# VectorE instead of GpSimd for the low parts of weight units in the dilated attention

## The chip, the cores and the metric

The kernel runs on one core of a Trainium2 chip. The metric is the time of one execution on the device, in microseconds (us). The kernel before took 3922.28 us, the median of three runs (3920.53 to 3923.07).

## The reference, cut to what matters

The program is two transformer blocks one after the other. The change lies in the second layer of the first block, the dilated mixture attention: for 512 tokens, 16 heads of width 64 and three dilations (1, 4, 16) it computes

```python
qkv = (h @ w_qkv).reshape(b, s, N_GROUPS_B, 3, H_B, HEAD_DIM)
# per dilation group: softmax attention in a band, with a distance bias per head
o, lse = banded_attention(q, k, v, slopes, dil, win // (2 * dil), BLOCK_B)
# mixture of the three groups by the softmax of their log denominators
wts = jax.nn.softmax(jnp.stack(lses), axis=0)
o = jnp.einsum('gbsh,gbshd->bshd', wts, jnp.stack(outs).astype(jnp.float32))
return o.astype(h.dtype).reshape(b, s, H_B * HEAD_DIM) @ w_out
```

The kernel takes the three groups together in one softmax over 768 keys: 512 of the first group, 128 each of the other two. All products with weights are of float32 quality: each operand is split in a high part (rounded to the type fp32r) and a low part (the rest), and a product is three matmuls, high by high, low by high and high by low.

## The kernel before, in words

Weights come from HBM in units of 128 x 2048 numbers (1 MB). `Weights.feed` on the SyncE queue loads them into a ring of four buffers; a buffer is loaded again when the unit in it is used up (`used`). Of each unit ScalarE writes the high part to one of two buffers (`write_hi`, L71), and GpSimd writes the low part, ring minus high part, in place over the ring buffer (`write_lo`, L76). TensorE waits for the low part (`parts`), which implies the high part.

The stage "att_b" (`attention_stage` with a `project`) does two things at once. It projects queries and keys for 8 pairs of heads: 6 chunks a pair, a chunk being 24 matmuls of 512 columns (8 blocks, three products each, L122 to L124) into PSUM bank 7. A unit holds 2 chunks, so a pair takes 3 units and the stage 24. VectorE copies each chunk out of bank 7 with scaling (`ProjectB.copy`, L828 for even chunks, L830 for odd ones), and TensorE may not begin the next chunk before that copy (`pair_chunk_copied`), since there is one bank. And it does the softmax attention of 32 items, 4 to a pair (a pair of heads and one residue tile of 128 queries).

The chunks of pair 0 stand ahead of the items (the prologue). While the 4 items of pair p run, the 6 chunks of pair p+1 are laid between them: 0 and 1 in item 0 of the pair, 2 in item 1, 3 and 4 in item 2, 5 in item 3 (`chunks_after`). The items of the last pair have no chunks beside them.

The order on each engine is fixed by the program. In step i:

- TensorE: scores of item i (L674), values of item i-3 (L656), a chunk, transposes of half 0 of item i-2 (L644), the second chunk if there is one, transposes of half 1.
- VectorE: bias and maximum of both halves of item i (L718), the negated maximum (L721), reciprocal and scaling of item i-1 (L697, L701), copy of the output of item i-3 (L706), then the copies of the chunks.
- ScalarE: the exponentials of item i (L744), the high part of the unit after the one that an even chunk uses (`unit_of`), the copies of the transposed probabilities of item i-2 (L759).
- GpSimd: nothing but the 24 low parts, in a loop of its own: each waits only for its high part.

Of the kernel before, what the change touches and what calls it, by code (L numbers as in the profile page):

```python
# [559 lines left out]
def attention_stage(nc, c, w, items, name, sink, project=None):  # L560
# [13 lines left out]
    with ExitStack() as ctx:  # L574
# [15 lines left out]
        def S(i, half):  # L590
            return c.bank[2 * half + i % 2] if DEEP == 2 else c.wide[half]
# [4 lines left out]
        def chunks_after(i):  # L596

            if not project or i >= N:
                return []
            pair, j = i // in_pair + 1, i % in_pair  # L600
            at = [n for n in range(per) if n * in_pair // per == j]
            return [(pair, n) for n in at] if pair < pairs else []

        def unit_of(pair, j):

            n = (pair * per + j) // 2 + 1
            return n if j % 2 == 0 and n < project.units else None

        with nc.Block() as block:
            if project:  # L610
                @block.sync
                def _(sp):
                    w.feed(sp, project.units)

            if project:
                @block.gpsimd
                def _(pool):
                    for n in range(project.units):
                        w.write_lo(pool, hi_ready, lo_ready, 0, n)

            @block.tensor
            def _(pe):
                def pair_chunk(pair, j):
# [63 lines left out]
            @block.vector  # L687
            def _(dve):
                def scale_of(i):

                    dve.wait_ge(prob_ready, 2 * i + 2)
                    if sink is not None:
                        dve.wait_ge(sunk_ready, i + 1)
                        dve.tensor_tensor(total[:, i, :], den[:, i, :], sunk[:, i, :], ALU.add).then_inc(total_ready, 1)
                        dve.wait_ge(total_ready, i + 1)
                    src = den if sink is None else total
                    dve.reciprocal(rden[:, i, :], src[:, i, :]).then_inc(rden_ready, 1)  # L697
                    dve.wait_ge(rden_ready, i + 1)
                    keys = items[i].keys
                    for half in HALVES:  # L700
                        dve.tensor_scalar(prob[:, i % SB, half, 0:keys], prob[:, i % SB, half, 0:keys], rden[:, i, half:half + 1], None,  # L701
                                          ALU.mult).then_inc(prob_scaled, 1)

                def copy_out(i):
                    dve.wait_ge(out_done, i + 1)
                    dve.tensor_copy(items[i].out, O[:, 0:P]).then_inc(out_copied, 1)  # L706

                for j in range(per):
                    project.copy(dve, w, 0, j, pair_chunk_done, pair_chunk_copied)
                for i in range(N + LAG + 1):  # L710
                    if i < N:
                        it = items[i]
                        dve.wait_ge(scores_done, i + 1)
                        if i >= SB:

                            dve.wait_ge(turned, 2 * (i - SB) + 2)
                        for half in HALVES:
                            dve.tensor_tensor_reduce(prob[:, i % SB, half, 0:it.keys], S(i, half)[:, 0:it.keys], it.dist, -it.slopes[half],  # L718
                                                     -3e38, ALU.add, ALU.max, top[:, i, half:half + 1]).then_inc(biased, 1)
                        dve.wait_ge(biased, 2 * i + 2)  # L720
                        dve.tensor_scalar(negtop[:, i, :], top[:, i, :], -1.0, None, ALU.mult).then_inc(negtop_ready, 1)  # L721
                        if sink is not None:
                            at = it.heads[0]
                            dve.tensor_tensor(sunk[:, i, :], sink[:, at:it.heads[1] + 1:it.heads[1] - at], top[:, i, :],
                                              ALU.subtract).then_inc(sink_shifted, 1)
                    if 0 <= i - LAG + 1 < N:
                        scale_of(i - LAG + 1)
                    if i >= LAG + 1:
                        copy_out(i - LAG - 1)
                    for chunk in chunks_after(i):  # L730
                        project.copy(dve, w, *chunk, pair_chunk_done, pair_chunk_copied)

            @block.scalar
# [2188 lines left out]
def first_block(nc, c, w, a, x, upto, dump):  # L2922
    with ExitStack() as first:
# [4 lines left out]
        with ExitStack() as layer:  # L2928
            def sl(n, shape):
                return layer.enter_context(nc.sbuf_tensor(n, shape, F32))  # L2930
            q, k_, v, o = sl("q_a", [P, DC, T]), sl("k_a", [P, 2, T]), sl("v_a", [P, TT, 2 * P]), sl("o_a", [P, DC, T])
            dist, sink, scale = sl("dist_a", [P, 3 * P]), sl("sink", [P, HEADS]), sl("q_scale_a", [P, DC])
            project_a_stage(nc, c, w, h, x, COLS["norm_mix0"], q, k_, v, (scale[:, :], a["q_scale_a"]),
                            [(dist[:, :], a["dist_a"]), (sink[:, :], a["sink"].partition_broadcast(P))])
            attention_stage(nc, c, w, attention_a_items(q, k_, v, dist, o), "att_a", sink)
            out_stage(nc, c, w, o, h, x, "out_a")
# [5 lines left out]
        with ExitStack() as layer:  # L2942
            def sl(n, shape, dt=F32):
                return layer.enter_context(nc.sbuf_tensor(n, shape, dt))
            v = sl("v_b", [P, 3, TT, D])

            kept, o = nc.dram_tensor("x_kept", [P, DC, T], F32, kind="Internal").ap(), x
            qk = [sl(f"qk{i}", [P, 6, T]) for i in range(2)]
            dist, scale = sl("dist_b", [P, TT, T + 2 * P], mybir.dt.bfloat16), sl("q_scale_b", [P, DC])
            values_b_stage(nc, c, w, h, x, COLS["norm_mix1"], v,  # L2950
                           (dist[:, :, :], a["dist_b"]), [(scale[:, :], a["q_scale_b"]), (kept, x[:, :, :])])
            attention_stage(nc, c, w, attention_b_items(qk, v, dist, o), "att_b", None, ProjectB(c, h, qk, scale))
            out_stage(nc, c, w, o, h, x, "out_b", kept)
# [231 lines left out]
```

## Time and profile before

| | |
|---|---|
| median of three runs | 3922.28 us |
| the profiled execution's own time | 3915.05 us |
| its span, first to last instruction | 3913.0 us |
| TensorE busy | 3301.5 us, 84% |
| VectorE busy | 1998.2 us, 51% |
| ScalarE busy | 1310.5 us, 33% |
| GpSimd busy | 927.4 us, 24% |
| mean granted TensorE clock | 0.898 of full |
| the stage att_b | from about 793.6 to 1272 us of the span |

The shares are averages over many stages with different limits. Matmuls are pipelined: a row shows about 0.40 us for one of 512 columns, while in a stream at full clock one starts every 0.23 us. In a timeline row the figures are start, duration, engine, line and operation; in brackets stands the idle time of the engine just before it and who ended it.

### The profile page before, as it was taken

Reading aid. Unit: us, or ns where it says so; the run is one execution under the profiler, and the core shown is the slowest. Engines: PE = TensorE matmul, PEld = TensorE weight load, DVE = VectorE, ACT = ScalarE, POOL = GpSimd, SP = SyncE. Lnnn points to the kernel's source line nnn. Section 1 sums busy time; section 2 is a strip of 40 time slices with the busy share of each in tenths; the row PEclk is TensorE's granted clock in tenths of the full one; section 3 lists DMA queues with packets and bytes.
Section 4 is the critical chain, followed back from the end, with each engine's and each line's share of the span. In section 5 each row is a group of like instructions: output and inputs, shape, how many; then the busy total and the mean of one; then the engine's idle time right before and its main releaser. Section 6 shows DMA issues by size and latency. Waiting matters only on the chain. (4 is left out here: it accounts for less than half of the span.)

```text
span 3913.0 us, 53828 instructions
## 1 busy us (share of the span) xinstructions
PE 3301.5 (84%) x21896; PEld 2576.2 (66%) x21896; DVE 1998.2 (51%) x2721; ACT 1310.5 (33%) x1631; POOL 927.4 (24%) x485
## 2 busy tenths in 40 slices
PE   7789999989998799988599688439998747999994
PEld 5468877967776588753387576228887336888882
DVE  3755523023333565220498244656554327999994
ACT  2633222223333333210322101422212116777772
POOL 2034433332220344310122100000100003435540
PEclk9989999999999899998799755559999868999996
DMA  3012223221110222227011000130011117999993
GB/s 123 12 64 89 95 86 124 86 75 56 55 65 33 76 97 96 86 99 264 25 65 54 4 1 8 43 136 24 24 46 66 43 47 267 357 370 372 370 363 122
DMA packets 75667, 439.22 MB, mean 112 GB/s; under 512 B 15148, under 2 KB 16300, under 8 KB 26708
## 3 DMA queue, kind: packets, MB, share of 16 engines
q1 hardware_dynamic: 65716, 426.97, 29.6%
q0 software_dynamic: 9760, 9.47, 0.7%
q8 instruction: 148, 2.42, 0.3%
q14 instruction: 43, 0.35, 0.0%
HBM read 419.47 MB, written 37.89 MB: 117 GB/s over the span
## 5 line engine op out<-in xcount | busy, mean ns | idle before, releaser
L76 POOL TENSOR_TENSOR ring_lo<-ring,unit_hi 128x2048 fp32r<-128x2048 f32 x116 | 537.0, 4631 | 1170.9 <-ACT unit_hi L71 1170.9
L122 PE MATMUL wide<-h_hi,unit_hi 128*128 128x512 f32 x1296 | 521.3, 402 | 89.6 <-DVE h_lo L182 44.0
L124 PE MATMUL wide<-h_hi,ring_lo 128*128 128x512 f32 x1296 | 520.0, 401 | 0.0
L123 PE MATMUL wide<-h_lo,unit_hi 128*128 128x512 f32 x1296 | 519.3, 401 | 0.0
L2642 DVE TENSOR_TENSOR ex_w_lo<-ring,ex_w_hi 128x2048 fp32r<-128x2048 f32 x192 | 437.4, 2288 | 45.2 <-ACT ex_w_hi L2597 43.8
L2597 ACT CAST ex_w_hi<-ring 128x2048 fp32r<-128x2048 f32 x192 | 365.9, 1911 | 110.8 <-DMA ring<-in_weights 102.3
L71 ACT CAST unit_hi<-ring 128x2048 fp32r<-128x2048 f32 x116 | 220.4, 1900 | 462.1 <-PE wide L124 453.7
L122 PEld LDWEIGHTS wide<-h_hi,unit_hi 128*128 128x128 f32 x1296 | 251.4, 194 | 168.5 <-POOL ring_lo L76 60.1
L123 PEld LDWEIGHTS wide<-h_lo,unit_hi 128*128 128x128 f32 x1296 | 247.6, 191 | 53.4 <-issue 0.2
L124 PEld LDWEIGHTS wide<-h_hi,ring_lo 128*128 128x128 f32 x1296 | 247.3, 191 | 53.4
L383 DVE TENSOR_TENSOR ffn_hidden_lo<-ffn_whole,ffn_hidden_hi 128x512 f32 (+1 forms) x44 | 201.5, 4581 | 50.5 <-ACT ffn_hidden_hi L358 50.5
L2541 PE MATMUL wide<-ex_w_hi,ex_x_hi 128*128 128x512 f32 x512 | 204.6, 400 | 10.4 <-DVE ex_x_lo L2647 10.0
L2543 PE MATMUL wide<-ex_w_hi,ex_x_lo 128*128 128x512 f32 x512 | 201.1, 393 | 0.0
L2542 PE MATMUL wide<-ex_w_lo,ex_x_hi 128*128 128x512 f32 x512 | 200.6, 392 | 0.0
L122 PE MATMUL wide<-in_hi,in_unit_hi 128*128 128x512 f32 (+3 forms) x424 | 147.6, 348 | 34.5 <-POOL ring_lo L76 34.5
L2500 POOL TENSOR_TENSOR ex_held<-ex_blank 128x1 f32<-128x1 f32 x64 | 89.8, 1403 | 320.0 <-DVE ex_results L2668 317.5
L1204 DVE SCALAR_TENSOR_TENSOR conv<-grid,cols,conv 128x512 f32<-128x512 f32 x160 | 158.2, 989 | 3.5
L122 PE MATMUL wide<-ffn_hidden_hi,unit_hi 128*128 128x512 f32 x352 | 141.0, 400 | 14.4 <-issue 14.4
L124 PE MATMUL wide<-in_hi,ring_lo 128*128 128x512 f32 (+3 forms) x424 | 146.4, 345 | 0.0
L124 PE MATMUL wide<-ffn_hidden_hi,ring_lo 128*128 128x512 f32 x352 | 141.0, 401 | 0.0
L123 PE MATMUL wide<-ffn_hidden_lo,unit_hi 128*128 128x512 f32 x352 | 140.4, 399 | 0.0
L2001 DVE COPY_PREDICATED rw_X<-level_mask,wide 128x256 f32<-128x256 uint32 x120 | 53.2, 443 | 148.2 <-PE wide L1857 147.7
(492 smaller groups left out, 6528.7 us busy)
## 6 DMA issues: line engine op xcount, KB each, us to landing
ring<-in_weights SPq DMA_DIRECT2D x356, 1024.0 KB, 5.6
factors<-rf_out SPq DMA_DIRECT2D x8, 1536.0 KB, 5.5
rw_F<-factors SPq DMA_DIRECT2D x12, 1024.0 KB, 6.0
cb_both<-pair_rows_out SPq DMA_DIRECT2D x4, 1024.0 KB, 4.8
x<-in_x SPq DMA_DIRECT2D x1, 2048.0 KB, 7.5
x_kept<-x SPq DMA_DIRECT2D x1, 2048.0 KB, 12.2
x<-x_kept SPq DMA_DIRECT2D x1, 2048.0 KB, 9.0
conv<-x SPq DMA_DIRECT2D x1, 2048.0 KB, 11.7
```

The costliest lines, as they stand in the source:

```text
L71: act.copy(self.hi[n % 2][:, :], self.ring[n % RING][:, :]).then_inc(hi_ready, 1)
L76: pool.tensor_tensor(self.lo[n % RING][:, :], self.ring[n % RING][:, :], self.hi[n % 2][:, :].bitcast(F32), ALU.subtract).then_inc(lo_read ...
L122: pe.matmul(dst, a[0], b[0], start=start, stop=False)
L123: pe.matmul(dst, a[0], b[1], start=False, stop=False)
L124: return pe.matmul(dst, a[1], b[0], start=False, stop=stop)
L383: dve.tensor_tensor(hidden[1][:, j * RING + i, :], whole[:, i % 2, :], hidden[0][:, j * RING + i, :].bitcast(F32), ALU.subtract).then_inc( ...
L1204: dve.scalar_tensor_tensor(out=go, in0=shifted(dy, dx), scalar=weight(dy, dx), in1=go, op0=ALU.mult, op1=ALU.add).then_inc(convolved, 1)
L2541: pe.matmul(dst, a_hi, b_hi, start=first, stop=False)
L2542: pe.matmul(dst, a_hi, b_lo, start=False, stop=False)
L2543: return pe.matmul(dst, a_lo, b_hi, start=False, stop=last)
L2597: act.copy(w_hi[at % RING][:, :], w.ring[n % RING][:, :]).then_inc(hi_ready, 1)
L2642: dve.tensor_tensor(w_lo[at % RING][:, :], w.ring[n % RING][:, :], w_hi[at % RING][:, :].bitcast(F32), ALU.subtract).then_inc(w.used, 1)
```

## The change

The loop on GpSimd is taken out of the stage, and the same 24 subtractions are issued by VectorE, inside its own program: units 0 to 3 in the prologue, and then unit 3p+1 before the copy of chunk 0 of pair p, 3p+2 before the copy of chunk 2, and 3p+3 before the copy of chunk 4. ScalarE's and TensorE's programs are as before. The other stages still have their low parts written by GpSimd (or, with the experts, by VectorE already).

```diff
-            if project:
-                @block.gpsimd
-                def _(pool):
-                    for n in range(project.units):
-                        w.write_lo(pool, hi_ready, lo_ready, 0, n)
-
@@ VectorE's program
+                if project:
+                    w.write_lo(dve, hi_ready, lo_ready, 0, 0)
                 for j in range(per):
+                    if j % 2 == 0:
+                        w.write_lo(dve, hi_ready, lo_ready, 0, j // 2 + 1)
                     project.copy(dve, w, 0, j, pair_chunk_done, pair_chunk_copied)
@@ VectorE's program, at the end of step i
                     for chunk in chunks_after(i):
+                        if unit_of(*chunk):
+                            w.write_lo(dve, hi_ready, lo_ready, 0, unit_of(*chunk))
                         project.copy(dve, w, *chunk, pair_chunk_done, pair_chunk_copied)
```

## Rows read from the trace of the kernel before

**Rows 1.** Windows: busy time (instructions) by engine, then clock and DMA.

```profile
804.30:849.00 44.70, 37.94 (x157) 28.75 (x157) 6.14 (x6) 5.09 (x3) 13.78 (x4) 0.96 0.16 56
...
1005.91:1061.23 55.32, 52.13 (x337) 41.04 (x336) 20.41 (x42) 19.58 (x27) 13.80 (x3) 1.00 0.16 57
```

**Rows 2.** Who waited for whom, 790 to 1275 us: total, times, longest.

```profile
PE wide L122 <- POOL ring_lo L76: 10.8, 1, 10.8
...
PE wide L122 <- DVE qk L828: 8.3, 10, 1.2
```

**Rows 3.** Timeline of the stage's start.

```profile
797.83 3.70 ACT L71 CAST unit_hi<-ring 128x2048 fp32r<-128x2048 f32 x2 [0.34 <-PEq L845]
799.81 9.04 POOL L76 TENSOR_TENSOR ring_lo<-ring,unit_hi 128x2048 fp32r<-128x2048 f32 x2 [22.17 <-ACT unit_hi L71]
...
804.36 0.80 PE L122 MATMUL wide<-h_hi,unit_hi 128*128 128x512 f32 x1 [10.81 <-POOL ring_lo L76]
```

**Rows 4.** The same subtraction on VectorE, experts: min/median/max ns; two timeline rows.

```profile
L2642 DVE TENSOR_TENSOR ex_w_lo<-ring,ex_w_hi x192: 2277/2285/2353, 3240.6 to 3826.6; 128x2048 fp32r<-128x2048 f32 x192
...
3406.45 2.29 DVE L2642 TENSOR_TENSOR ex_w_lo<-ring,ex_w_hi 128x2048 fp32r<-128x2048 f32 x1
3408.65 1.22 DVE L2647 TENSOR_TENSOR ex_x_lo<-wide,ex_x_hi 128x1024 fp32r<-128x1024 f32 x1
```

**Rows 5.** Timeline, first item of a pair in steady state.

```profile
1011.47 1.89 ACT L71 CAST unit_hi<-ring 128x2048 fp32r<-128x2048 f32 x1
...
1013.44 4.61 POOL L76 TENSOR_TENSOR ring_lo<-ring,unit_hi 128x2048 fp32r<-128x2048 f32 x1 [19.68 <-ACT unit_hi L71]
...
1014.74 1.15 DVE L828 SCALAR_TENSOR_TENSOR qk<-wide,q_scale_b,rstd 128x512 f32<-128x512 f32 x1 [3.61 <-PE wide L124]
...
1015.94 0.50 PE L122 MATMUL wide<-h_hi,unit_hi 128*128 128x512 f32 x1 [0.58 <-DVE qk L828]
```

**Rows 6.** Timeline, second and third item of that pair.

```profile
1029.87 4.56 POOL L76 TENSOR_TENSOR ring_lo<-ring,unit_hi 128x2048 fp32r<-128x2048 f32 x1 [11.81 <-ACT unit_hi L71]
...
1031.17 1.15 DVE L828 SCALAR_TENSOR_TENSOR qk<-wide,q_scale_b,rstd 128x512 f32<-128x512 f32 x1 [3.61 <-PE wide L124]
...
1036.56 0.50 PE L122 MATMUL wide<-h_hi,unit_hi 128*128 128x512 f32 x1
...
1049.43 1.14 DVE L828 SCALAR_TENSOR_TENSOR qk<-wide,q_scale_b,rstd 128x512 f32<-128x512 f32 x1 [5.92 <-PE wide L124]
```

**Rows 7.** Timeline, items 0 and 1 of the stage.

```profile
854.86 1.13 DVE L828 SCALAR_TENSOR_TENSOR qk<-wide,q_scale_b,rstd 128x512 f32<-128x512 f32 x1 [3.71 <-PE wide L124]
...
855.00 4.58 POOL L76 TENSOR_TENSOR ring_lo<-ring,unit_hi 128x2048 fp32r<-128x2048 f32 x1 [16.00 <-ACT unit_hi L71]
...
856.04 0.50 PE L122 MATMUL wide<-h_hi,unit_hi 128*128 128x512 f32 x1 [1.22 <-DVE qk L828]
...
869.18 1.14 DVE L828 SCALAR_TENSOR_TENSOR qk<-wide,q_scale_b,rstd 128x512 f32<-128x512 f32 x1 [2.44 <-PE wide L124]
...
869.34 4.60 POOL L76 TENSOR_TENSOR ring_lo<-ring,unit_hi 128x2048 fp32r<-128x2048 f32 x1 [9.75 <-ACT unit_hi L71]
...
870.57 0.50 PE L122 MATMUL wide<-h_hi,unit_hi 128*128 128x512 f32 x1
```

**Rows 8.** Timeline, VectorE's negated maximum: once beside GpSimd, once without.

```profile
872.57 1.40 DVE L721 TENSOR_SCALAR att_b_negtop<-att_b_top 128x2 f32<-128x2 f32 x1
...
1009.41 0.17 DVE L721 TENSOR_SCALAR att_b_negtop<-att_b_top 128x2 f32<-128x2 f32 x1
```

**Rows 9.** TensorE behind idle stretches, stage's end: timeline and one window (clock third from the end).

```profile
1233.69 0.99 PE L644 MATMUL wide<-ident,att_b_prob 128*128 128x128 f32 x6 [2.64 <-ACT att_b_probT L759]
1234.62 2.93 PE L674 MATMUL wide<-qk 64*128 64x512 f32 x12
...
1235.00:1237.00 2.00, 2.00 (x10) 0.97 (x10) 0.00 (x0) 0.52 (x1) 0.00 (x0) 0.50 0.04 12
...
1249.71 0.85 PE L644 MATMUL wide<-ident,att_b_prob 128*128 128x128 f32 x6 [2.64 <-ACT att_b_probT L759]
```

## The prediction

> **What bounds the kernel now.** I read the page first: TensorE is busy most of the span, GpSimd a quarter, but the stages have different limits, so only the stage with the change counts. The page's chain of waits ends in the last layer norm and never reaches this stage, so it tells nothing here. Next the table by windows. In four items of the steady state, 55.32 us, TensorE has 52.13 us of work at full clock, VectorE 20.41 and GpSimd 13.80 [rows 1]. TensorE is the bound, and what the change is worth is what it does to TensorE's gaps. VectorE has room for three more subtractions in a period (3 x 2.2 = 6.6 us); the question is not how much it has to do but whether it is late at the places where TensorE waits for it.
>
> The table of waits gives the gaps that the change can touch. TensorE waited once for a low part, 10.8 us, at the stage's start, and ten times for the copy of an even chunk, 8.3 us together [rows 2]. After the start GpSimd's low parts, 4.6 us each, made nobody wait. The reader should see that a unit's low part is needed only when the unit before it is used up, two chunks after its high part could be written, while a chunk's copy is needed at once when a second chunk follows in the same item, as there is one PSUM bank. The change moves the work from an engine on which it could wait freely to one whose next instruction may be that copy.
>
> **Price of a subtraction on VectorE.** No row shows it in this stage, in place. The same shape, with ring buffer and high part as inputs, stands 192 times in the experts' stage: 2.28 to 2.35 us, and the instruction behind it, of which the input lies in PSUM as with our copies, starts 2.20 us after it (3406.45 to 3408.65) [rows 4]. I take 2.20 as the pitch, 2.28 until a waiting engine sees the result. Ends: 2.20 and 2.27 (the longest of the 192, less the same 0.08), which over the eight places below is at most 0.6 us more. The 4.6 us of GpSimd is the other row of the shape, but of another engine, and I exclude it.
>
> **The start.** ScalarE writes the high parts of units 0 and 1 from 797.83; GpSimd starts at 799.81 and takes 9.04 us for two, so 4.5 for the first, and TensorE begins at 804.36 [rows 3]. VectorE is idle there and can start at 799.81 too; the low part is there at 802.1: 2.2 us sooner. Unit 1 follows until 804.3, before anything else is due on VectorE. The first matmuls run at half clock: the first row is 0.80 us [rows 3], and a mean clock of 0.96 over 44.7 us is 44.7 x 0.04 x 2 = 3.6 us at half [rows 1]. If the rise comes as long after the first matmul as before, the gain is 2.2 whole; if it comes at the same moment as before, the matmuls moved ahead run at half clock, and the gain is 1.1; if the clock never fell it would be 2.2 + 3.6/2 = 4.0. I take -2.2 and keep -1.1 and -4.0.
>
> The subtractions for units 2 and 3 in the prologue stand behind the copy of an odd chunk and before the copy of the next even one. That is the pattern of the third item below, and costs nothing.
>
> **First item of a pair, steady state.** The high part starts at 1011.47, behind the exponentials, and GpSimd starts at 1013.44. Chunk 0 is done and its copy starts at 1014.74, and TensorE, which had the transposes of half 0 to do until then, starts chunk 1 at 1015.94, after 0.58 us of waiting for this copy [rows 5]. Now the subtraction stands ahead of the copy, and it cannot start before 1013.44, since it waits for the high part. So the copy starts at 1013.44 + 2.20 = 15.64 instead of 14.74: 0.90 us late, and since TensorE waited already, chunk 1 is 0.90 us late. Behind it TensorE, ScalarE and VectorE wait only for each other's work of this stretch, so the whole train moves by 0.90. It happens for the pairs 2 to 7, where GpSimd's start and the copy stand 1.30 us apart each time: 6 x 0.90 = +5.4 us.
>
> **Second and third item.** In the second the subtraction would run from 1029.87 to 1032.07, and the copy of chunk 2 is 0.90 late as well (1031.17), ending at 1033.2. But chunk 3 begins at 1036.56, behind two sets of transposes, scores and values [rows 6]: hidden, with 3.3 us to spare. What is queued behind it on VectorE is the next item's bias step, which needs scores that come later. In the third item the high part waits for chunk 3 to be done, and VectorE has 5.92 us idle before the copy of chunk 4 at 1049.43 [rows 6]: a pause that takes the cast (1.9) and the subtraction (2.3). The cost is nothing; if the pause fell under 4.2 us it would come onto the path. The fourth item has no subtraction. The loads are issued when a unit is used, so SyncE's queue only moves with the rest.
>
> **Items 0 and 1 of the stage.** Here the pipeline is not full: no values or transposes stand between the chunks. In item 0 the copy started at 854.86 and GpSimd only at 855.00; now the copy starts at 857.20, 2.34 us late, and TensorE, which already waited 1.22 us for it, goes with it: +2.3. In item 1 the copy of chunk 2, at 869.18, comes at 869.34 + 2.20 = 871.54 and ends at 872.68, while chunk 3 began at 870.57 [rows 7]. TensorE starts it at 872.73: +2.2. The bias step of item 2 stands behind this copy and is late by 1.9 us too, but its result is needed only after chunk 3.
>
> **The sum.** -2.2 + 5.4 + 2.3 + 2.2 = +7.7 us. The profiled execution took 3915.05 us, so it would take 3922.8. It is itself 7.2 us below the median of the runs shown; I put the difference on the median: 3922.28 + 7.7 = 3930.0.
>
> **What speaks for a gain.** VectorE's negated maximum took 1.40 us at 872.57 and ended when GpSimd's subtraction did (869.34 + 4.60); at 1009.41, without GpSimd, it took 0.17 [rows 7, 8]. So VectorE can be held up by GpSimd, and this goes. The Trainium skill ("GPSIMD Engine Reference", Key points) says that the two share their SBUF interfaces, so that VectorE instructions in a two-port mode or with two SBUF inputs contend; by that rule this trace agrees. In a steady period GpSimd's subtractions lie where VectorE reads PSUM or idles, and the one hold-up has chunk 3 running over it. By the row it is worth nothing on TensorE's path; if all 1.2 us of it were, the sum would be +6.5.
>
> **What speaks for a larger loss.** In item 0 TensorE would now idle 1.22 + 2.34 = 3.6 us. At the stage's end it idled 2.64 us before 1233.69, and the clock in the window behind is 0.50; it idled 2.64 before 1249.71 and kept it [rows 9]. So a gap of this size can cost the clock. The price: at half clock the twelve score matmuls took 2.93 us [rows 9], of which half is loss, about 1.5. The Trainium skill ("TensorE: Matmul & The Clock Gate", Why this matters for your kernels) advises against idle gaps between bursts of matmuls for this reason. By that rule the sum would be +9.2; it speaks against this change, and I make it a rival.
>
> **The rivals.**
> A. The clock falls once in item 0 (or item 1, where the new gap is 2.2 us): +7.7 + 1.5 = +9.2, 3931.5. For it: the row at 1233.69. Against: the row at 1249.71, and that both sides of the gap are dense matmuls.
> B. Not slower: the late copies don't carry through. The mechanism would be that TensorE's 0.58 us in the first item has another cause behind the copy, such as ScalarE's copy of the transposes, which comes 0.9 us or more later than the trace lets see; then the slips vanish, and the early start and the freed interface remain: -2.2 - 1.2 = -3.4, 3918.9. It decides from the point at which that other wait is 0.90 us longer than the copy. Against: TensorE starts 0.05 us after the copy's end (1014.74 + 1.15 = 15.89, and 15.94).
> C. The subtractions cost more on VectorE than in the experts' stage, or the second and third item's come onto the path. Each late copy of an even chunk shown then costs 0.9: 7 second items besides give 7.7 + 6.3 = +14, 3936.
> D. The change doesn't shift TensorE's work as said: the start's gain and the first items' losses cancel and the 0.9 is partly absorbed: +2 to +4, 3925.
>
> **How the numbers follow.** My sum 0.50, A 0.24, B 0.08, C 0.08, D 0.10. The range for 8 in 10 reaches from D's lower end to beyond A: the start gives -1.8 to +1.1, the pitch up to +0.6, A up to +1.5 and a second fall 1.5, the runs' own scatter 1.3: 3922.5 to 3935. What a measurement of this kernel can tell from no change is about 0.2%, 7.8 us, and the sum lies on that line. I count slower by more for half of my own case less a little (0.24), most of A (0.20) and all of C: 0.52. Faster by more than 0.2% needs -7.8, more than B gives: 0.05 for what I don't see. Within: 0.43.
>
> **What would show it.** Right: TensorE's first matmul of the stage 2.2 us after where ScalarE's first cast ends plus 0.1; its waits for the copies of even chunks up from 8.3 to about 18 us, with 1.5 us in each first item of a pair; the four-item period 56.2 us instead of 55.3; subtractions at 2.28 us; no GpSimd row in the stage. Wrong: a period of 55.3; a window at half clock near 858 or 872; a gap before chunk 3 or 4 in the steady state; any subtraction over 2.4 us.

## The result, and the profile after

The changed kernel took 3931.23 us, the median of 12 runs, against 3920.83 us of the kernel before, also 12 runs: a ratio of 1.0026, 95% interval 1.0018 to 1.0035. Two later series of the same pair gave 1.0017 (1.0004 to 1.0031) and 1.0026 (1.0014 to 1.0038). By the medians it is slower by 10.4, 6.3 and 9.1 us, around the 0.2% where the prediction put it. Single executions of either kernel lie up to 15 us from their median, so for each term I go by the traces.

The profiled execution took 3934.07 us, with a span of 3932.0. That is 19 us over that of before, and only part of it belongs here: 1.3 us are there when the stage begins, 13.0 arise in the stage, 4.7 behind it in programs that are the same.

The rows of the subtraction, changed kernel (count: min/median/max ns, first and last start):

```profile
L76 POOL TENSOR_TENSOR ring_lo<-ring,unit_hi x92: 4495/4620/5129, 13.7 to 1718.4; 128x2048 fp32r<-128x2048 f32 x92
L76 DVE TENSOR_TENSOR ring_lo<-ring,unit_hi x24: 2284/2293/2294, 801.1 to 1205.2; 128x2048 fp32r<-128x2048 f32 x24
```

All 24 run on VectorE in 2.28 to 2.29 us, as those of the experts did [rows 4]. The waits of the stage, changed kernel (785 to 1300 us), answer to [rows 2]:

```profile
PE wide L122 <- DVE qk L828: 17.6, 11, 3.5
...
PE wide L122 <- DVE ring_lo L76: 8.6, 1, 8.6
```

TensorE waits for the first low part 8.6 us instead of 10.8, and for the copies of even chunks 17.6 instead of 8.3. The steady state, changed kernel, in the order cast, subtraction, copy, next chunk; it answers to [rows 5]:

```profile
1017.60 1.89 ACT L71 CAST unit_hi<-ring 128x2048 fp32r<-128x2048 f32 x1
...
1019.52 2.29 DVE L76 TENSOR_TENSOR ring_lo<-ring,unit_hi 128x2048 fp32r<-128x2048 f32 x1 [2.26 <-ACT unit_hi L71]
1021.73 1.11 DVE L828 SCALAR_TENSOR_TENSOR qk<-wide,q_scale_b,rstd 128x512 f32<-128x512 f32 x1
...
1022.89 0.50 PE L122 MATMUL wide<-h_hi,unit_hi 128*128 128x512 f32 x1 [1.41 <-DVE qk L828]
```

The copy has no idle time in brackets any more: it starts when the subtraction lets it, 2.21 us behind its start. TensorE's idle time before chunk 1 went from 0.58 to 1.41 us. One window of a whole period, changed kernel, answers to the second of [rows 1]:

```profile
1020.00:1076.15 56.15, 52.14 (x338) 41.09 (x337) 27.06 (x46) 19.57 (x27) 0.00 (x0) 1.00 0.16 57
```

The period, from the copy of a pair's chunk 0 to the next pair's, is 56.15 us instead of 55.34, TensorE's work in it the same, VectorE's 6.65 us more, GpSimd's nothing. Items 0 and 1, changed kernel, answer to [rows 7]:

```profile
855.10 2.29 DVE L76 TENSOR_TENSOR ring_lo<-ring,unit_hi 128x2048 fp32r<-128x2048 f32 x1 [3.80 <-ACT unit_hi L71]
857.31 1.10 DVE L828 SCALAR_TENSOR_TENSOR qk<-wide,q_scale_b,rstd 128x512 f32<-128x512 f32 x1
...
858.46 0.50 PE L122 MATMUL wide<-h_hi,unit_hi 128*128 128x512 f32 x1 [3.51 <-DVE qk L828]
...
875.06 0.50 PE L122 MATMUL wide<-h_hi,unit_hi 128*128 128x512 f32 x1 [2.02 <-DVE qk L828]
```

The start of the stage, changed kernel, answers to [rows 3]:

```profile
799.16 3.70 ACT L71 CAST unit_hi<-ring 128x2048 fp32r<-128x2048 f32 x2 [0.34 <-PEq L845]
...
803.44 0.79 PE L122 MATMUL wide<-h_hi,unit_hi 128*128 128x512 f32 x1 [8.56 <-DVE ring_lo L76]
...
808.30 0.63 PE L124 MATMUL wide<-h_hi,ring_lo 128*128 128x512 f32 x1
808.73 0.51 PE L122 MATMUL wide<-h_hi,unit_hi 128*128 128x512 f32 x1
```

The first matmul is 4.28 us behind the start of the cast; before, 804.36 - 797.83 = 6.53. But the half clock lasts: the rows keep the spacing of half clock (0.43 us) until 808.7, 5.3 us behind the first matmul.

To compare many traces I cut the stage by marks that each has. Its beginning is the start of ScalarE's last copies of the values stage (793.59 before, 794.92 changed). The projection part ends with the start of VectorE's copy of the last chunk; the tail goes from there to the start of the last output copy. Rows from the tail, changed kernel:

```profile
1243.10 1.51 PE L638 MATMUL wide<-ident,att_b_prob 128*128 128x128 f32 x6 [2.64 <-ACT att_b_probT L759]
1244.55 2.93 PE L668 MATMUL wide<-qk 64*128 64x512 f32 x12
```

These are at half clock behind an idle stretch of 2.64 us, as one was in [rows 9]. The whole tail as one window (clock third from the end), kernel before and changed kernel:

```profile
1224.80:1271.83 47.03, 30.70 (x300) 23.27 (x298) 17.28 (x43) 18.51 (x30) 0.00 (x0) 0.93 0.07 23
1234.20:1286.16 51.96, 36.49 (x300) 28.00 (x298) 17.27 (x42) 18.49 (x30) 0.00 (x0) 0.81 0.07 21
```

TensorE's 300 matmuls are the same in both and take 5.8 us more at the lower clock; the other engines' work is equal within 0.02 us. The marks of all kernels that ran (us; copy 0 is the start of the first chunk's copy; item 0 is the copy of pair 1's chunk 0 behind that of pair 0's; item 1 the same from pair 1 to pair 2; then the period):

| kernel | copy 0 | item 0 | item 1 | period | projection part | tail |
|---|---|---|---|---|---|---|
| before | 18.11 | 43.15 | 49.21 | 55.34 | 431.21 | 47.02 |
| changed | 16.88 | 45.47 | 52.11 | 56.15 | 439.28 | 51.96 |
| before_again | 18.21 | 43.18 | 49.18 | 55.33 | 431.21 | 49.88 |
| after_again | 16.94 | 45.47 | 52.13 | 56.15 | 439.34 | 52.03 |
| after_third | 16.88 | 45.50 | 52.12 | 56.16 | 439.28 | 49.17 |
| copy_first | 17.04 | 43.14 | 49.18 | 55.31 | 429.94 | 45.08 |
| copy_first_but_third | 16.95 | 43.20 | 49.16 | 55.30 | 429.85 | 45.19 |
| prologue_only | 16.92 | 43.13 | 49.19 | 55.33 | 429.92 | 50.90 |
| items_only | 18.28 | 45.48 | 53.69 | 56.15 | 442.28 | 49.06 |
| first_item_only | 19.26 | 45.49 | 52.40 | 56.16 | 442.06 | 48.31 |
| halves | 16.37 | 44.41 | 51.23 | 55.30 | 432.57 | 50.69 |
| before_filled | 18.12 | 43.14 | 49.19 | 55.34 | 431.22 | 44.16 |
| after_filled | 16.97 | 45.47 | 52.12 | 56.15 | 439.37 | 45.71 |
| third_filled | 14.38 | 43.17 | 49.17 | 55.30 | 427.28 | 44.18 |

Where the clock is not involved, a mark repeats within 0.1 us, so differences of 0.8 us can be told in a single trace, while the medians of a dozen runs gave 10.4, 6.3 and 9.1 us for one and the same difference.

### The profile page after: what moved, and what is told of

Read it like the earlier page. It is cut to its first block and busy times, and to the rows that moved or that the text cites. A ratio compares the mean times of both kernels' runs of the same rounds, so it can differ in the third digit from the quotient of the medians.

```text
span 3932.0 us, 53828 instructions
## 1 busy us (share of the span) xinstructions
PE 3312.1 (84%) x21896; PEld 2584.5 (66%) x21896; DVE 2050.6 (52%) x2745; ACT 1310.3 (33%) x1631; POOL 808.3 (21%) x461
## 5 line engine op out<-in xcount | busy, mean ns | idle before, releaser
L76 POOL TENSOR_TENSOR ring_lo<-ring,unit_hi 128x2048 fp32r<-128x2048 f32 x92 | 426.5, 4638 | 1296.0 <-ACT unit_hi L71 1296.0
L122 PEld LDWEIGHTS wide<-h_hi,unit_hi 128*128 128x128 f32 x1296 | 251.6, 194 | 176.7 <-POOL ring_lo L76 49.2
```

What stands on the lines that cost most here:

```text
L76: pool.tensor_tensor(self.lo[n % RING][:, :], self.ring[n % RING][:, :], self.hi[n % 2][:, :].bitcast(F32), ALU.subtract).then_inc(lo_read ...
L122: pe.matmul(dst, a[0], b[0], start=start, stop=False)
```

## The experiments

Theory 1 is that of the prediction: the subtraction ahead of a copy makes TensorE wait. The rivals are VectorE's load as such, and the clock.

**The subtraction behind the copy.** All 24 stay on VectorE.

```diff
 for chunk in chunks_after(i):
+    project.copy(dve, w, *chunk, pair_chunk_done, pair_chunk_copied)
     if unit_of(*chunk):
         w.write_lo(dve, hi_ready, lo_ready, 0, unit_of(*chunk))
-    project.copy(dve, w, *chunk, pair_chunk_done, pair_chunk_copied)
```

> In the items VectorE copies an even chunk first and subtracts behind the copy; the prologue is as in the change. Theory 1 (late copies): all 24 subtractions stay on VectorE but none is ahead of a copy that TensorE waits for, so the projection part loses all of +2.3, +2.1 and 6 x 0.82 and keeps the start's gain: 431.2 - 1.2 = 430.0 us (429 if the clock at the start comes better), period of four items 55.3, time 1 to 3 us below the kernel before. Rival (load or interface: VectorE with 55 us more work, or the clock, makes it longer wherever the subtraction stands): projection part stays above 435 us, time 8 to 11 above.

Ratio 0.9998 (0.9988 to 1.0008), projection part 429.94 us, period 55.31. The rows, copy first (pair 2, item 0):

```profile
903.97 1.12 DVE L828 SCALAR_TENSOR_TENSOR qk<-wide,q_scale_b,rstd 128x512 f32<-128x512 f32 x1 [3.61 <-PE wide L124]
905.01 2.28 DVE L76 TENSOR_TENSOR ring_lo<-ring,unit_hi 128x2048 fp32r<-128x2048 f32 x1
911.01 0.69 DVE L830 TENSOR_TENSOR qk<-wide,rstd 128x512 f32<-128x512 f32 x1 [3.72 <-PE wide L124]
...
905.15 0.50 PE L122 MATMUL wide<-h_hi,unit_hi 128*128 128x512 f32 x1 [0.56 <-DVE qk L828]
```

The same instruction on the same engine, one place further down, runs under chunk 1: the copy waits for TensorE again and TensorE only 0.56 us for the copy. This shows that the loss comes from the order of two instructions and neither from the load nor from the engine. The gain that was expected in time, 1 to 3 us, is there in the trace (1.27 us) but too small for the runs to show.

**Copy first, but for chunk 4.**

```diff
 for chunk in chunks_after(i):
+    unit, third = unit_of(*chunk), chunk[1] == 4
+    if unit and third: w.write_lo(...)
     project.copy(dve, w, *chunk, pair_chunk_done, pair_chunk_copied)
+    if unit and not third: w.write_lo(...)
```

> Copy first for chunks 0 and 2, subtraction first for chunk 4, where VectorE idles 5.9 us anyway. Theory 1: projection part 430.0 us, as with copy first everywhere; with copy first everywhere the bias step of the fourth item is 1.1 us late, here it is not, and both should be hidden, so the two should not differ by more than 0.2 us in the projection part. Rival (a late bias step carries through): this one is up to 7 x 1.1 us shorter.

Ratio 0.9998 (0.9987 to 1.0009), projection part 429.85, 0.09 from the last one. A bias step that is 1.1 us late in the fourth item is hidden.

**Each part alone.** The two parts of the change, and then the first items alone. The units written by VectorE have a semaphore of their own here (`on_dve` picks the engine).

```diff
+def on_dve(n): return n < 4                    # prologue_only
+def on_dve(n): return n >= 4                   # items_only
+def on_dve(n): return n >= 4 and n % 3 == 1    # first_item_only
```

> VectorE subtracts for units 0 to 3 (prologue), GpSimd for the other 20. Theory 1: the first matmul of the stage comes 2.2 us earlier behind the values stage (8.5 instead of 10.8), of which the projection part shows 1.2 (430.0) to 2.2 (429.0), the rest being matmuls at half clock; time 1 to 2 us below the kernel before. Rival (the gain at the start is always eaten by the clock): projection part 431.2, time the same.

Ratio 1.0001 (0.9992 to 1.0010), projection part 429.92: 1.29 us less, the lower of the two values expected. It and copy first agree within 0.02 us, so the start's gain is all that VectorE's subtractions bring. Its size hangs on the clock: the first matmul comes 8.52 us into the stage instead of 10.77, and half clock lasts 5.3 us behind it instead of 3.2.

> GpSimd subtracts for units 0 to 3, VectorE for the 20 of the items, ahead of the copies as in the change. Theory 1: projection part 431.2 + 2.3 + 2.1 + 4.9 = 440.5 us, first matmul 10.8 us behind the values stage; time 9 to 11 above the kernel before, a little above the changed kernel. Rival (half of the loss lies in the tail or elsewhere): projection part below 437.

Ratio 1.0031 (1.0021 to 1.0041). The projection part is 442.28 us, not 440.5. Item 0 (+2.3) and the period (+0.81) are as expected; the 1.6 us too much sit in item 1's mark, and the windows of this kernel show what they are (clock third from the end):

```profile
855.00:858.00 3.00, 0.65 (x3) 0.57 (x4) 2.30 (x2) 0.00 (x0) 0.00 (x0) 1.00 0.00 0
858.00:861.00 3.00, 3.00 (x9) 2.32 (x8) 0.00 (x0) 0.00 (x0) 0.00 (x0) 0.51 0.00 0
```

The idle 3.51 us in item 0, which end at 857.35 in this trace, were followed by half clock, and the 24 matmuls of chunk 1 took longer. This is rival A.

> VectorE subtracts only for the unit ahead of chunk 0 of pairs 1 to 7 (7 units), GpSimd for the other 17. Theory 1: the loss of item 0 (+2.3) and six times 0.82: projection part 431.2 + 2.3 + 4.9 = 438.4 us, period 56.15. Rival (the period grows by VectorE's load, three subtractions, 0.27 each): period 55.6, projection part 434.

Ratio 1.0020 (1.0008 to 1.0031). The period is 56.16 us with one subtraction of VectorE in it instead of three, so the load is ruled out, and all of the steady loss comes from chunk 0's. The projection part is 442.06, 3.7 over what was expected. The start took 1.1 us longer (copy 0 at 19.26): it is the start of the kernel before, with the first matmul again 10.77 us into the stage, but half clock lasted 5.7 us behind it instead of 3.2. And item 1's mark is 52.40 where 49.21 + 0.82 was due, 2.4 us for rival A again:

```profile
858.00:861.00 3.00, 2.25 (x5) 1.84 (x6) 0.70 (x1) 0.00 (x0) 0.00 (x0) 0.50 0.00 0
861.00:864.00 3.00, 3.00 (x8) 2.34 (x7) 0.00 (x0) 0.00 (x0) 0.00 (x0) 0.50 0.00 0
864.00:867.00 3.00, 3.00 (x15) 2.18 (x13) 0.00 (x0) 0.00 (x0) 0.00 (x0) 1.00 0.00 0
```

**Half of the work ahead of the copy.** The subtractions for chunks 2 and 4 stay as in the change.

```diff
+if unit and chunk[1] == 0: w.write_lo_half(dve, ..., unit, 0)   # columns 0 to 1023
 project.copy(dve, w, *chunk, pair_chunk_done, pair_chunk_copied)
+if unit and chunk[1] == 0: w.write_lo_half(dve, ..., unit, 1)   # columns 1024 to 2047
```

> As the change, but the subtraction ahead of chunk 0 of a pair is cut in two: the first 1024 columns before the copy, the other 1024 behind it. Estimate for 1024 columns: 1.14 us pitch (half of 2.13, the 2048 columns' share of 2.20, plus the fixed 0.07). Theory 1, with its threshold: in the steady state the copy can start 1.30 us after the high part is ready, and 1.14 is less, so the slip vanishes whole, not by half: period 55.3 us; item 0 keeps 1.3 of 2.3, item 1 its 2.1; projection part 431.2 - 1.2 + 1.3 + 2.1 = 433.4. Rival (the loss is proportional to the work ahead of the copy): period 55.7, projection part 436.

Period 55.30: the steady loss is gone whole, item 0 keeps 1.26 and item 1 2.0; projection part 432.57, expected 433.4 (the start was 0.5 better). So there is a threshold, the 1.30 us from where the high part can be used to the end of the chunk, and only what goes beyond it costs time. The half subtraction took 1.23 us and the copy followed 1.35 us behind its start (902.40 to 903.75), later than my 1.14:

```profile
902.40 1.23 DVE L83 TENSOR_TENSOR ring_lo<-ring,unit_hi 128x1024 fp32r<-128x1024 f32 x1 [2.27 <-ACT unit_hi L71]
903.75 1.13 DVE L842 SCALAR_TENSOR_TENSOR qk<-wide,q_scale_b,rstd 128x512 f32<-128x512 f32 x1
```

That is the chunk's end and not the subtraction's. The ratio, 1.0015 (1.0002 to 1.0028), is more than the projection part's 1.4 us give; with this series' scatter the time can't settle it.

**Both kernels again.**

> The kernel before, once more. Theory 1: projection part 431.2 us within 1.2 (half clock at the start), tail anywhere from 47 to 52, as the clock falls in its idle stretches or not. Theory 2 (the longer tail belongs to the change): tail 47 within 0.5 us. Time ratio 1.000.

> The changed kernel once more, for the scatter of what lies outside the change. Marks: the projection part runs from ScalarE's last copy of the values stage to VectorE's copy of the last chunk (before 431.2 us, changed 439.3), the tail from there to the last output copy (before 47.0, changed 52.0). Theory 1 (late copies): the projection part is 439.3 again within 1.2 us (the start's clock may shift it), since every term of it is fixed by the order on VectorE; the tail is free to come out anywhere from 47 to 52, because its 4.9 us more were only TensorE's clock falling in more of the idle stretches. Theory 2 (the tail is part of the change): the tail is 52 again within 0.5 us. Time: 9 to 11 us over the kernel before by either.

> The changed kernel a third time. Its tail was 52.0 us in both profiles so far, while kernels with the same program in the tail showed 45.1 to 50.9. Theory 1 (the tail is scatter of the clock): anywhere from 45 to 52, and a third 52.0 would speak against it. Theory 2 (the change makes the tail long): 52.0 within 0.3. Projection part 439.3, or 441 to 442 if the clock falls in item 0's idle 3.5 us, as it did in two of four kernels with that gap.

The ratio of the kernel before to itself was 0.9998 (0.9988 to 1.0008). The projection parts came back within 0.06 us. The tails are 47.0 and 49.9 of before, and 52.0, 52.0 and 49.2 of the changed one. That two were 52.0 had me doubt, and the third spoke for scatter; three against two profiles don't prove it. One piece even repeats: by the granted clock in windows of 1 us, the first stretch of half clock in the tail lasted 6.8 us in all three traces of the changed kernel and 3.4 us in both of before. That the tail's excess is the clock is shown; that the change has no share in when it falls is not.

**Idle work for TensorE in the tail.** If the tail's excess is the clock, matmuls that nobody reads should remove it from both.

```diff
+def fill(pe, count):
+    for _ in range(count):
+        pe.matmul(c.bank[7][:, :], project.h[0][:, 0, 0:P], project.h[0][:, 0, :], start=True, stop=True)
 if LAG <= i < N + LAG:
     transposes(i - LAG, 0)
+if project and i >= N - in_pair:
+    fill(pe, 6 if i < N else 4)
```

> The kernel before with idle work for TensorE in the tail: in each step from the first item of the last pair on, 6 matmuls (4 in the last three steps) of h by h into the idle bank 7, read by nobody, between the transposes of half 0 and those of half 1. If the tail's excess over 45.1 us is TensorE's clock falling in idle stretches, the tail is 45 to 46 us; projection part 431.2; time 2 to 5 us below the kernel before. If the excess has another cause, the tail stays at 47 to 52 or grows by the matmuls' time.

> The changed kernel with the same idle work in the tail. Theory 1: the tail is 45 to 46 us too, the same as that of the kernel before with idle work within 0.3, and the two differ only in the projection part, 439.3 (or 441 to 442 with a fallen clock in item 0) against 431.2: by 8 to 10 us in time. Theory 2 (the change lengthens the tail through something else): tail above 48.

Against the kernel before: 0.9992 (0.9983 to 1.0002) and 1.0011 (0.9998 to 1.0024). The tails are 44.16 and 45.71 us; of the 11 without idle work two are at 45.1 and 45.2, one at 47.0 and eight from 48.3 to 52.0. They differ by more than the 0.3 I expected, by 1.55 us, and this has one place, the values of one late item of the changed kernel, which took 2.83 us where the next took 1.53:

```profile
1265.10 2.83 PE L654 MATMUL wide<-att_b_probT,v_b 128*64 128x128 f32 x24 [0.89 <-ACT att_b_probT L765]
...
1271.73 1.53 PE L654 MATMUL wide<-att_b_probT,v_b 128*64 128x128 f32 x24 [0.89 <-ACT att_b_probT L765]
```

The mean granted clock over the tail goes from 0.93 to 1.00 for the kernel before and from 0.81 to 0.96 for the changed one. So the tail's 4.9 us in the first comparison were the clock's, and filled they shrink to one such place. Between the two filled kernels the medians differ by 6.7 us (3923.24 and 3916.51), the projection parts by 8.15.

**The best of it.** Copy first but for chunk 4, the tail filled, and `fill(pe, 8)` ahead of the stage's first chunk.

> Copy first but for chunk 4, with the idle work in the tail, and 8 matmuls of idle work more ahead of the stage's first chunk, while TensorE waits for unit 0's low part. Tail 45 to 46 us. At the start, if the idle matmuls hold or raise the clock before the first chunk, the first copy comes up to 2.4 us sooner behind the values stage (14.5 instead of 16.9) and the projection part is 427.5 to 429.9. Time against the kernel before: -1.3 (start) to -3.7, and -3 to -5 for the tail, together 4 to 9 us below. The rival (TensorE's clock falls later all the same, idle work only moves it): 0 to 2 below.

Ratio 0.9990 (0.9981 to 0.9999), 3916.58 us: 4 us faster than before, the only one with its interval below 1, if barely. But the kernel before with nothing but the tail filled took 3916.51 us in the same series, so the time doesn't show that anything but the filled tail brings a gain; for the 3.9 us of the projection part (427.28 and 431.22) there is only the trace. The idle work at the start:

```profile
798.73 3.55 PE L617 MATMUL wide<-h_hi 128*128 128x512 f32 x8 [4.25 <-PEq L856]
803.04 0.50 PE L122 MATMUL wide<-h_hi,unit_hi 128*128 128x512 f32 x1 [0.75 <-DVE ring_lo L76]
803.37 0.39 PE L123 MATMUL wide<-h_lo,unit_hi 128*128 128x512 f32 x1
```

The eight idle matmuls took the half clock on themselves, and the first chunk ran at full clock: copy 0 at 14.38 us instead of 16.9. The stage, projection part and tail, takes 471.5 us, 6.8 and 9.6 less than in the two traces of before; the runs give 4. The rest is lost in the scatter of the other stages or given back there, and I can't tell which.

## Why the prediction was right

The forecast was +7.7 us as a sum for the trace, 3930.0 us in time; measured were 3931.23 us and, by the marks, 8.07 us in the projection part. That the two times lie 1.2 us apart is partly luck: the sum stood on a median of three runs that was 1.45 us above that of twelve, and the tail, where nothing was priced, moved too. The mechanism is what held, a copy made late by the subtraction ahead of it. Step by step:

- **Price of a subtraction**: 2.20 us taken, 2.21 measured (1019.52 to 1021.73), in place or not.
- **The start**: -2.2 taken, and the first matmul did come 2.25 us sooner. But of the bounds the upper one, -1.1, was the case: by the first copy only 1.23 us are left (18.11 and 16.88), and 1.1 to 1.2 in each other kernel with VectorE in the prologue but halves (1.74) and the one with idle work at the start. The half clock lasted 5.3 us instead of the 3.2 of before (until 807.5 there), so the matmuls that were moved ahead ran at half speed. This is the term that I mis-sized, by 1.0 us. Nor is it a fixed price: behind a first matmul at 10.77 us half clock lasted 3.2 us in three traces, 3.6 in items_only and 5.7 in first_item_only, and behind one at 8.52 us 4.4 us in halves and 5.3 to 5.7 in the others without idle work at the start.
- **First item, steady state**: 6 x 0.90 taken, 6 x 0.82 measured. VectorE took the cast's result 0.05 us sooner than GpSimd (1.92 us behind the cast's start, not 1.97 [rows 5]), and its copy lets TensorE go 1.16 us behind its start, not 1.20. Why is not shown: in copy_first, where GpSimd is still too, it was 1.18 (903.97 to 905.15).
- **Items 0 and 1**: +2.34 and +2.16 taken, +2.32 and +2.08 measured.
- **Second and third item**: nothing taken; first_item_only shows the same period with them and without.
- **The sum**: -1.23 + 2.32 + 2.08 + 6 x 0.82 = 8.09 against 8.07 between the marks. The errors of -1.0 and +0.5 partly cancel.
- **Rival A** is real, with its place: the clock fell behind item 0's gap in two of the six traces that have a gap of 3.5 us (items_only, first_item_only), and cost 1.6 and 2.4 us, more than my 1.5. Not in the changed kernel's own three traces nor in after_filled. The two that fell have GpSimd in the prologue and so a later start, the four that did not have VectorE there; whether that decides it or chance was not tested. The Trainium skill ("TensorE: Matmul & The Clock Gate", Why this matters for your kernels) advises against such gaps; these traces agree, as something that can happen and need not.
- **Rival B** (not slower) falls: every wait that grew was one for a copy (17.6 us instead of 8.3), and the period grew by 0.81 of the 0.90 forecast. Freeing VectorE from GpSimd was worth nothing on TensorE's path: prologue_only, with GpSimd still busy in the items, and copy_first, with it idle, have the same projection part within 0.02 us. **C** and **D** fall by the row of 2.29 us and the period.
- What I had left out is the tail: I priced no change there, rightly for the program, but the clock in its idle stretches moves it by up to 7 us between kernels with the same program there (45.1 to 52.0), and by 2.9 between two traces of one kernel (47.0 and 49.9; 52.0 and 49.2): nearly as much as the change itself.

## What to carry to other kernels

On an engine that runs its instructions in order, ask of a moved instruction what the next one is and who waits for that; the engine's share of busy time doesn't answer it. A twice faster instruction made the kernel slower ahead of a copy and did no harm behind it. Measure small changes by marks in the trace around the place, and the term that a clock can touch separately.

## What the runs showed of the hardware

- Work that nobody reads can carry TensorE's half clock: eight such matmuls in a wait of 8.6 us brought the first chunk's copy 2.5 us forward, and four to six in each step of a stretch with idle gaps of 2.6 us brought 45.1 to 52.0 us down to 44.2 and 45.7.
- Behind gaps of 2.64 us in the tail the granted clock fell at some and stayed at others within one execution. Behind a gap of 3.51 us in item 0 it fell in two of six traces, of kernels that differ in their start.
- A first matmul 2.25 us earlier did not bring the full clock earlier: half clock lasted 5.3 us instead of 3.2. Over all traces it lasted from 3.2 to 5.7 us behind the first matmul.
